# Level masks applied to products of whole scores in the recurrent stage, and inversion levels 2 to 4 of TensorE written as a loop

## What is computed

```python
def step(S, inp):
    r_t, w_t, k_t, v_t, kk_t, a_t = inp
    sa = jnp.einsum('bhij,bhj->bhi', S, kk_t)
    S = (S * w_t[:, :, None, :] - sa[..., None] * (kk_t * a_t)[:, :, None, :]
         + v_t[..., None] * k_t[:, :, None, :])
    return S, jnp.einsum('bhij,bhj->bhi', S, r_t)
...
for (dec, kd, a), (dec_c, kd_c, a_c), rev in zip(dirs, dirs_c, (False, True)):
    s_ctx, y_c = wkv_scan(s0, rc, dec_c, kd_c, vc, kkc, a_c, rev)
    _, y = wkv_scan(s_ctx, r, dec, kd, v, kk, a, rev)
```

## Time and profile before

| | |
|---|---|
| median of three runs | 3412.66 us |
| the profiled execution | 3415.89 us |
| its span | 3414.1 us |
| instructions | 67,095 |
| TensorE busy | 3246.4 us, 95% |
| VectorE busy | 1818.7 us, 53% |
| ScalarE busy | 1166.7 us, 34% |
| GpSimd busy | 515.7 us, 15% |
| granted TensorE clock, mean | 0.983 |

### The profile page before, as it was taken

How to read it: one execution, slowest core, us unless ns; L and a number is a source line. 1 busy time by engine, 2 the same in 40 slices (tenths; PEclk the granted TensorE clock), 3 DMA queues, 4 the chain that set the end, 5 groups by cost and what they waited for, 6 DMA issues and landing times. The chain is left out here.

```text
span 3414.1 us, 67095 instructions
## 1 busy us (share of the span) xinstructions
PE 3246.4 (95%) x28066; PEld 2771.1 (81%) x28066; DVE 1818.7 (53%) x2653; ACT 1166.7 (34%) x1855; POOL 515.7 (15%) x424
## 2 busy tenths in 40 slices
PE   6999999999988899999999999999999978899998
PEld 5888888886657778888888888888895767689897
DVE  4552554665675555543554553554565765555353
ACT  3331222225664333321222331222225653344231
POOL 2000002001607510000002000001102556220000
PEclk9999999999989999999999999999999998999999
DMA  5331221441000012222221232222342000023232
GB/s 203 94 103 60 92 97 63 137 158 65 2 17 4 4 56 80 92 96 76 92 86 56 92 97 82 86 92 74 113 132 78 2 19 3 28 86 95 90 92 92
DMA packets 68289, 263.64 MB, mean 77 GB/s; under 512 B 7552, under 2 KB 8704, under 8 KB 67456
## 3 DMA queue, kind: packets, MB, share of 16 engines
q1 hardware_dynamic: 67664, 256.95, 23.1%
q10 hardware_dynamic: 432, 3.88, 0.3%
HBM read 258.70 MB, written 2.10 MB: 76 GB/s over the span
## 5 line engine op out<-in xcount | busy, mean ns | idle before, releaser
L240 PE MATMUL ps<-hn_hi,w_hi 128*128 128x512 f32 (+1 forms) x3520 | 864.9, 327 | 17.7 <-DVE hn_lo L457 6.1
L240 PE MATMUL ps<-hn_hi,w_lo 128*128 128x512 f32 (+1 forms) x3520 | 865.2, 327 | 0.0
L240 PE MATMUL ps<-hn_lo,w_hi 128*128 128x512 f32 (+1 forms) x3520 | 860.7, 326 | 0.0
L217 ACT ACTIVATE w_hi<-raw 128x1024 fp32r<-128x1024 f32 (+1 forms) x300 | 338.6, 1129 | 1375.5 <-PE ps L240 1221.1
L222 DVE TENSOR_TENSOR w_lo<-raw,w_hi 128x1024 fp32r<-128x1024 f32 (+1 forms) x300 | 396.9, 1323 | 469.0 <-ACT w_hi L217 461.6
L240 PEld LDWEIGHTS ps<-hn_hi,w_hi 128*128 128x128 f32 x3520 | 547.8, 190 | 82.1 <-issue 17.7
L240 PEld LDWEIGHTS ps<-hn_lo,w_hi 128*128 128x128 f32 x3520 | 548.3, 190 | 58.2
L240 PEld LDWEIGHTS ps<-hn_hi,w_lo 128*128 128x128 f32 x3520 | 544.9, 190 | 57.8
L240 PE MATMUL ps<-g_lo,w_hi 128*128 128x512 f32 (+1 forms) x1424 | 404.2, 351 | 0.0
L240 PE MATMUL ps<-g_hi,w_hi 128*128 128x512 f32 (+1 forms) x1424 | 398.4, 347 | 6.1 <-DVE g_lo L894 6.1
L240 PE MATMUL ps<-g_hi,w_lo 128*128 128x512 f32 (+1 forms) x1424 | 398.7, 347 | 0.0
(11 more groups left out here) (273 smaller groups left out, 3904.9 us busy)
## 6 DMA issues: line engine op xcount, KB each, us to landing
raw<-wgu SPq DMA_DIRECT2D x176, 512.0 KB, 3.6
w_mod_one<-wmod SPq DMA_DIRECT2D x100, 512.0 KB, 3.6
raw<-wdn SPq DMA_DIRECT2D x64, 704.0 KB, 4.1
raw<-win SPq DMA_DIRECT2D x44, 512.0 KB, 4.7
w_mod_two<-wmod SPq DMA_DIRECT2D x28, 512.0 KB, 3.8
w_mod_first<-wmod_first SPq DMA_DIRECT2D x4, 2048.0 KB, 23.3
raw<-wout SPq DMA_DIRECT2D x16, 512.0 KB, 3.6
h<-xT ACTq DMA_DIRECT2D x1, 3072.0 KB, 8.4
```

The lines of the kernel that those rows point to most:

```text
L217: act.activation(w_hi[s][:, 0:kt, :].rearrange("p k n -> p (k n)"), raw[s][:, 0:kt * P], ACT.Copy).then_inc(hi_ready[s].sem, 1)
L240: mm = pe.matmul(out[:, o:o + b - a], w[:, k, :], m[:, k, a:b], start=(k == 0 and w is w_hi[s] and m is mov_hi), stop=(k == kt - 1 and w i ...
```

## The change

Functions and constants are set in the kernel as follows.

- Instead of 18 masked copies a round, GpSimd adds the identity to the scores in place, once for each group (`add_diagonal`). TensorE multiplies the whole scores; VectorE multiplies the product with a mask that is the identity less the level's pattern, in the operation that subtracted from the identity before. `first_step` takes the whole scores too. `step_lo` is gone.
- Levels 2, 3 and 4 of TensorE are one body in a loop of three passes; waits on `x_ready`, `xt_ready` and `t_ready` have semaphores of their own for each group, and a value that depends on the pass.
- The first products of groups 0 and 1 stand at positions 9 and 10 of the state chain before; the score tiles at positions 2 to 7 instead of 2, 3, 5, 6, 8 and 9. VectorE's `add_outputs` stands in the next round.
- The values' products stand in level 5, behind each group's block product, in the upper half of the group's bank; VectorE copies them, a group at a time, and the step products of level 5 wait for that.
- V is turned and copied once for each pair of heads at the start of the stage, into two buffers. `turn(1)` stands behind the loop, `turn(2)` behind level 5 and `turn(3)` behind the products for w.
- VectorE makes one of the three copies into `neg_w`; GpSimd places the decay in `trans` (`place_decay`).
- The order of the exponentials and of the feature products is changed: the decay before a token comes last.

```diff
-        step_lo = [at(f"step_lo{i}", [P, UNITS, CH], R_W + k * TOK) for i, k in ((1, 4), (2, 5), (3, 6), (4, 7))]
-        step_lo.insert(0, at("step_lo0", [P, UNITS, CH], R_G + 3 * TOK))
-        v_rw = at("v_rw", [P, NTT, P], R_W + 10 * TOK)
...
-        x_ready, xt_ready, lo_masked = sem("x_ready"), sem("xt_ready"), sem("step_blocks_masked")
+        lx_ready, step_ready = sem("lx_ready"), sem("inv_step")
+        x_ready, xt_ready, t_ready = ([sem(f"{n}{g}") for g in range(3)] for n in ("x_ready", "xt_ready", "t_ready"))
+        diag_ready, inverted = sem("scores_with_diagonal"), sem("inverted")
+        decay_placed = sem("decay_placed")
...
+                eng.wait_ge(exps_out.sem, exps_out.at(5 * r + 1))
+                eng.tensor_tensor(rho, rho, u[:, R_OF + hp, Q], ALU.mult)
+                eng.wait_ge(exps_out.sem, exps_out.at(5 * r + 2))
+                link(eng.tensor_tensor(bk[:, 1, :], bk[:, 0, :], f[1][:, :], ALU.mult))
+                eng.tensor_tensor(bk[:, 0, :], bk[:, 0, :], f[2][:, :], ALU.mult)
+                eng.wait_ge(exps_out.sem, exps_out.at(5 * r + 3))
+                eng.tensor_tensor(ar[:, 0, :], ar[:, 0, :], kk_n[:, hp, :], ALU.mult).then_inc(features.sem, 1)
...
-            def blocks_until(r, li, g):
-
-                return r * BLOCKS + (li * GROUPS + g if r == 0 else g * LEVELS + li) + 1
-
-            def step_blocks(pool, r, li, g):
-
-                d = ROUNDS[r][1]
-                mask = masks[:, d, 5:6, :] if li == 0 else masks[:, 1 - d, 5 + li:6 + li, :]
+            def add_diagonal(pool, r, g):
+
+                eye = K_["ident2"][:, 0:CH].rearrange("p (a b) -> p a b", a=1).broadcast_to([P, UG, CH])
                 pool.wait_ge(wkv_masked.sem, wkv_masked.at(r * NTT + 2 * g + 2))
-                pool.tensor_tensor(step_lo[li][:, of_group(g), :], sc[:, of_group(g), 0, :], mask.broadcast_to([P, UG, CH]),
-                                   ALU.mult).then_inc(lo_masked.sem, 1)
+                pool.tensor_tensor(sc[:, of_group(g), 0, :], sc[:, of_group(g), 0, :], eye, ALU.add).then_inc(diag_ready.sem, 1)
+
+            def place_decay(pool, r):
+
+                i2 = K_["ident2"][:, 0:CH].rearrange("p (a b) -> p a b", a=1).broadcast_to([P, NCH, CH])
+                cd = chunk_decay[:, r % 2, :].rearrange("p (a b) -> p a b", b=1).broadcast_to([P, NCH, CH])
+                pool.wait_ge(exps_out.sem, exps_out.at(5 * r + 5))
+                if r >= 1:
+                    pool.wait_ge(state_ready.sem, state_ready.at(r * NCH))
+                pool.tensor_tensor(trans[:, :, :], i2, cd, ALU.mult).then_inc(decay_placed.sem, 1)
 
...
+                    def copy_values(hp):
+                        act.wait_ge(nat_turned.sem, nat_turned.at(hp + 1))
+                        act.activation(v_rw[hp][:, :, :].rearrange("p a b -> p (a b)"), slots[0], ACT.Copy).then_inc(nat_copied.sem, 1)
...
+                    def w_out(r, g):
+                        act.wait_ge(w_ready.sem, w_ready.at(GROUPS * r + g + 1))
+                        act.activation(neg_w[:, of_group(g), :], ps[:, 2 + g, :].rearrange("p (a b) -> p a b", b=P),
+                                       ACT.Copy, scale=-1.0).then_inc(w_copied.sem, 1)
...
+                        w_out(r, 0)
                         if more:
+                            decay_before(r + 1)
+                        w_out(r, 2)
...
+                    def block_product(r, k, g):
+
+                        pe.wait_ge(diag_ready.sem, diag_ready.at(GROUPS * r + g + 1))
+                        pe.wait_ge(x_ready[g].sem, k + x_ready[g].at(r * PER_GROUP + 1))
                         for i, n in enumerate(units(g)):
                             for b in range(2):
-                                mm = pe.matmul(in_bank(BANK_X[g])[hr(1 - b), i, :], step_lo[li][hr(b), n, :], x_inv[hr(b), n, :],
+                                mm = pe.matmul(in_bank(BANK_X[g])[hr(1 - b), i, :], sc[hr(b), n, 0, :], x_inv[hr(b), n, :],
                                                start=True, stop=True)
...
+                    def step_products(r, k, g, last=False):
+
+                        pe.wait_ge(*(mv_copied.sem, mv_copied.at(GROUPS * r + g + 1)) if last else
+                                   (x_ready[g].sem, x_ready[g].at(r * PER_GROUP + 1)))
+                        pe.wait_ge(t_ready[g].sem, k + t_ready[g].at(r * PER_GROUP + 1))
+                        if not last:
+                            pe.wait_ge(xt_ready[g].sem, k + xt_ready[g].at(r * PER_GROUP + 1))
...
+                    def values_product(r, g):
+
+                        pe.wait_ge(xt_ready[g].sem, xt_ready[g].at((r + 1) * PER_GROUP))
+                        for i, n in enumerate(units(g)):
+                            for b in range(2):
+                                mm = pe.matmul(ps[hr(b), BANK_XT[g], (UG + i) * CH:(UG + i + 1) * CH], sc[hr(b), n, 2, :],
+                                               v_rw[ROUNDS[r][0]][hr(b), n // 2, hr(n % 2)], start=True, stop=True)
+                        mm.then_inc(mv_ready.sem, 1)
...
+                    first_step(0, 0)
+                    first_step(0, 1)
                     for r, (hp, d) in enumerate(ROUNDS):
                         more = r + 1 < len(ROUNDS)
-                        for g in range(GROUPS):
-                            first_step(r, g)
+                        first_step(r, 2)
+                        block_product(r, 0, 0)
...
+                        block_product(r, 0, 2)
...
+                        with pe.Fori(1, LEVELS - 2) as k:
+                            pe.to_reg(k + x_ready[0].at(r * PER_GROUP + 1))
+                            for g in range(GROUPS):
+                                block_product(r, k, g)
+                            for g in range(GROUPS):
+                                step_products(r, k, g)
...
+                        turn(1)
...
+                            block_product(r, LEVELS - 2, g)
+                            values_product(r, g)
...
+                            step_products(r, LEVELS - 2, g, True)
+                        pe.wait_ge(*nat_done(r))
                         pe.wait_ge(features_end.sem, features_end.at(r + 1))
-                        turn(r, 2)
...
+                        pe.wait_ge(end_copied.sem, end_copied.at(2 * r + 1))
+                        turn(3)
                         pe.wait_ge(w_copied.sem, w_copied.at(GROUPS * (r + 1)))
-                        pe.wait_ge(end_copied.sem, end_copied.at(2 * r + 2))
...
-                        SCORES_AT = {2: 0, 3: 1, 5: 2, 6: 3, 8: 4, 9: 5}
+                        SCORES_AT = {2: 0, 3: 1, 4: 2, 5: 3, 6: 4, 7: 5}
+                        FIRST_AT = {9: 0, 10: 1}
...
+                            if more and i in FIRST_AT:
+                                first_step(r + 1, FIRST_AT[i])
...
+                    def level_mask(r, k):
+                        return masks[:, ROUNDS[r][1], 4 + k:5 + k, :].broadcast_to([P, UG, CH])
+
+                    def first_inverse(r, g):
+                        dve.wait_ge(lx_ready.sem, lx_ready.at(r * BLOCKS + g + 1))
+                        dve.tensor_tensor(x_inv[:, of_group(g), :], level_mask(r, 0), in_bank(BANK_X[g]),
+                                          ALU.mult).then_inc(x_ready[g].sem, 1)
+
+                    def first_transpose(r, g):
+                        dve.tensor_tensor(xt_inv[:, of_group(g), :], level_mask(r, 1), in_bank(BANK_XT[g]),
+                                          ALU.mult).then_inc(xt_ready[g].sem, 1)
+
...
-                        dve.tensor_tensor(lx[:, of_group(g), :], eye, in_bank(BANK_X[g]), ALU.subtract).then_inc(t_ready.sem, 1)
+                        dve.tensor_tensor(lx[:, of_group(g), :], level_mask(r, li + 1), in_bank(BANK_X[g]),
+                                          ALU.mult).then_inc(t_ready[g].sem, 1)
...
+                        if r >= 1:
+                            add_outputs(r - 1)
+                        first_inverse(r, 2)
+                        less_product(r, 1, 0)
+                        first_transpose(r, 2)
...
+                            values_out(r, g)
+                        end_out(r, 2, b_nat)
+                        dve.wait_ge(w_ready.sem, w_ready.at(GROUPS * r + 2))
+                        dve.tensor_scalar(neg_w[:, of_group(1), :], ps[:, 3, :].rearrange("p (a b) -> p a b", b=P), -1.0, None,
+                                          ALU.mult).then_inc(w_copied.sem, 1)
+                        end_out(r, 3, k_nat)
...
+                        dve.wait_ge(decay_placed.sem, decay_placed.at(r + 1))
...
-                            for li in range(LEVELS):
-                                step_blocks(pool, r, li, g)
+                            add_diagonal(pool, r, g)
+                        place_decay(pool, r)
...
-        M.append(np.stack([strict, incl, strict, incl, -1.0 * lv[0], -1.0 * lv[0].T] + lv[1:]))
```

(28 more changed lines are left out.)

203 lines of the change are left out of this document (72 added, 131 removed).

## The result

The kernel after takes 3367.32 us (median of four runs, 3365.18 to 3370.30) against 3413.51 for the kernel before beside it (3402.32 to 3414.62): a ratio of 0.9867, 95% interval 0.9852 to 0.9883, 46.2 us less. The forecast was 3374 in a range of 3356 to 3400. Timed twice more beside later experiments, the kernel after gave 0.9859 and 0.9848. Its three ratios lie 0.0019 apart, so between two groups of runs a difference of up to 0.2% (6 us) can't be told from nothing. The profiled execution took 3367.02 us, its span 3365.3, which is 48.8 under that of before.

A forecast was written before the change was run, and what follows sets the result against it. TensorE, busy 95% of the span, was taken to bound the kernel, so only its waits could give time back. Savings of 29.3 and 14.0 less 4.8 lost made 38.5 us; from 3412.66 that gives 3374, range 3356 to 3400.

The forecast's parts named there:

- piece one: From the end of the previous round to level 2: 87.7 us over eight rounds, forecast 58.4, 29.3 saved.
- piece two: Levels 2 to 5 with their transposes: 149.2 us over eight rounds, forecast 135.2, 14.0 saved.
- (a): Ahead of level 2: GpSimd's fewer masks end the 13.4 us wait and the slow clock behind it; 29.3 us saved.
- rival 4: Unrolled level 5 and w stay starved of instructions: at most 8 us, 3382; its chance is within the forecast's 0.70.
- (b): Levels 2 to 4 as a loop: 19 packets fewer, 3.4 us a level, 0.4 a round for taken branches.
- Rival 2: Levels take 3.0 us (-9.6) and the branches are hidden (-3.2): 3361 us; chance 0.08.
- rival 1: Levels stay at 3.8 us, paced by TensorE's sequencer or VectorE, without cover in the chain: 3388 us; chance 0.12.
- (c): Level 5: values' products behind each group's block product add 1.6 us; the level takes 4.7 a round.
- (d): Transposes: V turned twice a stage during TensorE's wait for features, no cost; two turns, 1.6 us, stay in levels 2-5.
- (e): Behind w's products: moved turn covers the 0.7 us copy wait, but 0.5 of new waiting follows; 4.8 us lost.
- (f), (g): ScalarE's and GpSimd's new order costs nothing, features ready some 4 us early; more semaphores, other buffers and banks move nothing.
- Rival 3: At the loops' 16 taken branches, the way back must fetch: whole 3438 us, chance 0.06; in part 3390, chance 0.04.

The follow-up runs named there:

- the two timings: Kernel after with first products of groups 0 and 1 put back behind the state chain, run twice: 3368.98 us (ratio 0.9861) and 3373.28 us (0.9879).
- run with two boundaries: Kernel after with its loop body shifted by TensorE filler to cross two packet boundaries in each of eight loops: 3391.16 us, ratio 0.9928.

## Why the prediction held, step by step

The sum was 38.5 us; 46.2 were measured. The three pieces got 11.8 us shorter than forecast: piece one saved 3.3 less, piece two 15.2 more. The errors are of opposite sign, and the code outside the pieces differs by several us from one profile to the next, so how near the whole came is in part luck. Cut at the common marks the prediction reads 60.2 us for piece one (58.4, and 4.2 of the chain's end, less 2.4 for group 0's products, which stand ahead of the mark now), 135.2 for piece two, and 7.2 more from w to the chain's end (4.8, and the same 2.4).

- **(a) GpSimd's wait and the slow clock.** Right. Piece one takes 63.5 where the cut gives 60.2. The 3.3 us are rival 4's: "issue" of 0.73 us ahead of a low-rank product in the third round, and in two other rounds stalls like it, 1.25 us in one and 0.37 and 1.63 in the other. Behind that wait the clock is 0.50 in the first step products of level 2, which is the granted clock of 0.89 of the second row of piece two:

```profile
1117.29:1119.88 2.59, 2.59 (x100) 2.59 (x96) 1.27 (x3) 0.77 (x2) 2.58 (x2) 0.50 0.00 0
```

  The cover of 0.8 us a round by the chain is the uncertain term: 0.9 to 1.0 by the rounds' lengths (5.3 and 6.2 us in six), while the two timings scatter around it.
- **(b) Levels.** The mechanism was right, and the size was off. I took 3.4 us a level and 0.4 for branches, 84.8 in all; the eight loops take 79.3, and 73.9 where nothing disturbs them. One level, answering to the earlier trace rows:

```profile
1078.85:1081.99 3.14, 3.01 (x144) 2.89 (x145) 2.54 (x7) 2.15 (x4) 1.02 (x1) 1.00 0.00 0
```

  3.14 with its branch: 0.13 us of idle time at the way back instead of 0.21 on top, and no wait for TensorE's sequencer. Rival 2 (3.0 and hidden branches) came nearest here, and rival 1 fell.
- **(c) Level 5.** The step that failed most. It had the values' products and the block products follow each other, at 1.6 us each. Alternating they took 1.93 together; with the values behind them, 2.62. Level 5 was priced at 4.7 and took 3.5, 1.2 us a round less and 9.7 in eight, of the 15.2 that piece two did better; the levels are the other 5.5. By the kernel's indices the two kinds use different quarters of the array, and the row of 97 records in 1.81 us was of the same two kinds interleaved: it already spoke against adding 1.6.
- **(d) Transposes.** Right: piece two keeps two of 0.8. The two turns of V at the start of a stage moved no mark there by over 0.6 us.
- **(e) Behind w.** 7.3 us for 7.2. The parts were less exact: the wait for k_nat was 0.2 us a round, not 0.5, since the chunk products ahead of it take 0.93 and not "some 0.5"; the earlier trace rows had them at 7.4 us in eight rounds. What it did not take went to "issue" at the local outputs, 2.9 us (L2156), a wait that the prediction had no term for.
- **(f), (g).** No wait for GpSimd is left in the stages, and the features are waited for at a stage's start alone.
- **Rival 3.** It fell in both its forms. The kernel after has 133 packets for 132 expected, and the run with two boundaries has no stall at a way back. The Trainium skill, "Runtime: NRT & Kernel Launch", section "Instruction fetch mechanics", says that a taken branch outside a window of two pages forces a fetch before the engine goes on. The run with two boundaries does not bear it out for a way back (at most 0.22 us of idle time); the branch forward over filler did stall.
- **Rival 4.** Priced at 8 us at most. "Issue" of the unrolled lines outside of the levels is some 9 us in the profile after, but the forecast for piece one and for the chain had part of it in its rows.

What remains open: why the timing and the profiles of the first products differ in one group of runs. No run undoes the masks on the products, the moved transposes or the shared copy for w by itself; what these bring is read from the waits that are gone, 5.6 us for w's copy, and not from an experiment of their own.

## What to carry to other kernels

Where an unrolled stretch of TensorE's code idles with "issue" and the table of queues shows a packet of instructions in 4 us, a loop over the repeated body pays about 1 us for each packet that it saves, as long as it takes no work along that had covered a wait. Look first for a wait on a side engine whose queue serves the wrong group first: reordering two loops on GpSimd was worth nearly as much as the loop (18.0 us for 22 to 24, by the stages). And price a wait of about 1 us on TensorE both with its own length and with the slower clock behind it, since the runs show both.

## What the runs showed that was not expected

- A branch forward over filler on TensorE's queue costs 2.5 us or so each (20 us in eight loops), in stalls and in the clock behind them. Two branches back over two packet boundaries cost nothing that shows, and a loop's idle time at its way back is 0.13 us.
- 96 records of two kinds, each using another half of the array, take 1.93 us when the kinds alternate by groups and 2.62 when they don't.
- Waits of 0.7 to 1.7 us of TensorE are followed by a stretch at a granted clock of 0.50 (1.2 GHz), 2.6 us and more, in some places and not in others: 0.73 us did it in the third round of layer 1, 1.63 us in the last round did not (3.39 us, at 1.00):

```profile
1151.98:1155.37 3.39, 1.76 (x103) 1.63 (x98) 1.55 (x5) 0.77 (x2) 0.00 (x0) 1.00 0.02 5
```
